# Second mixture of experts by indirect DMA, in 32-row blocks with the weights kept per column; the first norm in another order

## The chip, the cores and the metric

One core of one Trainium2 chip runs the whole program in one launch. The metric is the device time of the core in microseconds (us); lower is better. The time before is 2169.39 us, the median of three runs (2168.69 to 2171.74).

## The reference

Two transformer-like blocks run one after the other on 512 tokens of width 1024, all in float32. The first has an adaptive norm, a bidirectional mLSTM with a Fourier branch, and 16 experts that each choose 64 tokens. The second has a convolution branch, gated attention, cross attention and a mixture of 16 small experts in 4 groups; a last norm ends it. What the change touches is the start of the first block, and the mixture and the last norm of the second:

```
# first block, once for ctx (256 tokens, the modulation of c_ctx) and once for x (512 tokens, that of c)
mx = silu(c) @ w_ada + b_ada                     # 6 x 1024: shift, scale, gate, shift, scale, gate
px = (rmsnorm(x, g_norm1) * (1 + sc1) + sh1) @ w_in

# second block, last part: h = rmsnorm(x), 512 x 1024
p_group = softmax(h @ wg + bg);  g_star = argmax(p_group)           # one of 4 groups
p_exp = softmax(e_logits of that group);  top_v, top_i = top_k(p_exp, 2)
weights = p_group[g_star] * top_v / sum(top_v)                      # 2 experts of 16 for a token
a = h @ w_gate[e];  b = h @ w_up[e]                                 # 1024 x 256 each
y = sum over the two experts of (silu(a) * b * weight) @ w_down[e]  # 256 x 1024
out = rmsnorm(x + y, norm_final_g)
```

So 1024 pairs of a token and an expert are to be computed. An expert has 3 MB of weights (gate, up and down of 1 MB each), the 16 of them 48 MB.

## The kernel before

The order of the work on each engine is written out by hand, with semaphores between the engines. TensorE (PE) does all products, ScalarE (ACT) and VectorE (DVE) empty the PSUM banks, SyncE (SP) issues nearly all loads. The weights stream through `ring`, four slots of 2 MB (`weight_slots` in the profile). A slot is loaded again when the stage that used it is done. In the profile "bank" is a PSUM bank, "R" a work area (R1 to R7, and R14 which is R1 to R4), "SM" another, "C" the area C0, "H" the normed activations and "xT" the residual, both with the features on the partitions. `product` (L1529) is the helper for every plain product, so the rows of that line belong to many stages and are told apart by their operands.

**Start.** PE turns ctx and x so that the features lie on the partitions (L1538, L1545). It computes the modulation in four parts of 512 columns, `ada(0)` to `ada(3)` (L1560: eight products, four side by side in strips of 32 rows), and sums and turns each part (L1569, `ada_sum`). DVE adds the bias (L954). Parts 0 and 1 are the shift, parts 2 and 3 the scale, so the gains (L973) wait for all four. Then DVE scales ctx and x (L983), each with the reciprocal root from `root_inverse` (L959), for which PE must have summed the squares (`wide_sum`, L574 and L577). ACT adds the shift (L620 for ctx, L623 for x). Ahead of that, ACT issues nine small loads (L607 to L614) that later stages need. The product with `w_in` for the keys (L1529, H and weight_slots, first 256 columns of ctx) needs the shifted ctx.

**Second mixture.** PE turns h back to tokens on the partitions (L2033). ACT copies it twice (L884, and rounded L885), and GpSimd (POOL) forms the rest (L1514), so that h is there as the sum of a high and a low part in the faster number format of one pass. DVE picks the experts and gives each pair of token and expert a place: blocks of 64 rows belong to one expert each, and 1024 pairs need at most 31 blocks. The loop then always runs 16 times (`NPAIR2`), two blocks at a time, whatever the routing. For each pair of blocks:

- the rows are gathered by products with a 0/1 matrix (`gather_blocks`, L1529 with `picks`, 16 products of 512 columns), and turned (L2065)
- gate and up together (512 columns) are multiplied with the rows of both blocks side by side, in strips of 64 (L2099, 8 x 2 products); silu (L911, ACT) and the product with up (L1490, DVE); hidden turned (L2111)
- down (L2121, 4 x 2 products); the result is split in a high part (ACT, L924) and a low part (DVE, L1495)
- it is scattered to the tokens by products again (`scatter_tile`, L1529 with `GT_even` or `GT_odd`, 16 products) which stand between the gate and up products, and DVE adds it to xT (L1471, 8 additions)
- DVE makes the 0/1 matrix of the blocks to come (L1447, L1450) and the weights (L1456, L1458), and PE turns those (L2091)

SP reads the numbers of the experts from `block_expert` (L492) and loads the weights of each block (L498, L503) even where the expert stays the same. Gate and up are two blocks ahead in the ring, in runs of 1 KB; down is not double buffered. After the loop the last norm n6 runs over the partitions (L574, L577, L582, L585), PE turns the result (L2137), ACT copies it (L928), and SP writes it out (L537).

## Time and profile before

| | us |
|---|---|
| median of the runs | 2169.39 |
| profiled execution | 2166.3 |
| its span, first to last instruction | 2164.4 |
| PE busy in the span | 1996.4 |
| DVE, ACT, POOL busy | 733.9, 470.2, 12.6 |
| mean granted TensorE clock | 0.959 of full |

### The profile page before, as it was taken

To read this page: it belongs to the slowest core of one execution; us is meant where nothing else is said; L and a number is where in the kernel's file an instruction comes from. 1 tells how busy PE (TensorE), PEld (TensorE's weight loads), DVE (VectorE), ACT (ScalarE), POOL (GpSimd) and SP (SyncE) were. 2 spreads that over 40 slices of the span, in tenths; PEclk is the share of its full clock that TensorE was granted. 3 is DMA by queue.
4 is the path that set the end of the run, shared out by engine and by line. 5 is a ranking of instruction groups with operands and counts; after the bars stand their busy time and mean duration, and the time that the engine had idled before them with its cause. 6 is when DMAs were issued, how large, how long until landed. Compare 5 with 4: busy or idle time off the path is not lost.

```text
span 2164.4 us, 19621 instructions
## 1 busy us (share of the span) xinstructions
PE 1996.4 (92%) x7415; PEld 921.1 (43%) x7415; DVE 733.9 (34%) x1355; ACT 470.2 (22%) x845; POOL 12.6 (1%) x17
## 2 busy tenths in 40 slices
PE   6899999999899999999997997899997859999997
PEld 3544545544364444344433442344444334444443
DVE  3606205521231111111113695210212255455554
ACT  3211114420211110010112006530003222323223
POOL 0000000000000000000000000000000020000000
PEclk7999999999999999999998997999998969999999
DMA  9111443113238999999980211111200048878862
GB/s 371 28 66 39 173 177 136 39 59 117 78 122 349 422 417 419 422 422 422 423 345 18 72 66 39 40 39 62 72 22 0 0 151 289 296 273 288 293 233 78
DMA packets 151110, 399.03 MB, mean 184 GB/s; under 512 B 9284, under 2 KB 75156, under 8 KB 142868
## 3 DMA queue, kind: packets, MB, share of 16 engines
q1 hardware_dynamic: 144636, 393.40, 48.0%
q10 hardware_dynamic: 6424, 4.94, 0.7%
q8 instruction: 33, 0.54, 0.1%
q14 instruction: 17, 0.14, 0.0%
HBM read 396.23 MB, written 2.10 MB: 184 GB/s over the span
## 4 chain that ended last, share of the span: by engine, by line
PE 88%; DVE 4%; ACT 3%; issue 1%; DMA 1%; SPq 0%; DVEq 0%; ACTq 0%
PE bank L1529 49%; PE bank L1852 10%; PE bank L2099 6%; PE bank L1876 5%; PE bank L1827 3%; PE bank L1898 3%; PE bank L2121 3%; DVE SM L582 1%; PE bank L574 1%; PE bank L1980 1%; PE bank L2065 1%; PE bank L1605 1%; PE bank L1727 1%; PE bank L1560 1%; DMA weight_slots<-in_expert_w_up 1%
## 5 line engine op out<-in xcount | busy, mean ns | idle before, releaser
L1529 PE MATMUL bank<-H,weight_slots 128*128 128x512 f32 (+1 forms) x1088 | 450.0, 574 | 13.7 <-ACT H L620 12.5
L1529 PEld LDWEIGHTS bank<-H,weight_slots 128*128 128x128 f32 x1088 | 208.9, 193 | 252.6 <-issue 247.3
L1529 PE MATMUL bank<-R,weight_slots 128*128 128x512 f32 x576 | 249.1, 593 | 4.4 <-DVE R L1158 2.1
L1529 PEld LDWEIGHTS bank<-R,weight_slots 128*128 128x128 f32 x576 | 109.0, 190 | 141.6 <-issue 134.6
L1852 PE MATMUL bank<-weight_slots,SM 128*64 128x512 f32 x640 | 141.8, 593 | 6.8 <-DVE xT L1221 6.8
L2099 PE MATMUL bank<-weight_slots,SM 128*64 128x512 f32 x512 | 136.3, 622 | 5.6 <-DMA weight_slots<-in_expert_w_up 5.6
L1471 DVE TENSOR_TENSOR xT<-xT,bank 128x512 f32<-128x512 f32 x136 | 91.6, 686 | 78.8 <-PE bank L1529 78.8
L1876 PE MATMUL bank<-weight_slots,SM 128*64 128x512 f32 x384 | 111.6, 594 | 0.0
L1529 PE MATMUL bank<-R 128*128 128x128 f32 (+2 forms) x784 | 103.3, 287 | 3.2 <-ACT R L874 2.1
L1529 PEld LDWEIGHTS bank<-R 128*128 128x128 f32 x784 | 94.2, 195 | 7.1 <-issue 4.6
L1852 PEld LDWEIGHTS bank<-weight_slots,SM 128*64 128x64 f32 x640 | 45.4, 137 | 100.1 <-issue 86.7
L1231 DVE TENSOR_TENSOR R<-SM,bank 128x512 f32<-128x512 f32 x16 | 11.0, 686 | 212.8 <-PE bank L1852 212.8
L1529 PE MATMUL bank<-weight_slots,H 128*128 128x512 f32 x192 | 82.9, 592 | 0.0
L1260 DVE SCALAR_TENSOR_TENSOR R<-R,vec 128x512 f32<-128x512 f32 x120 | 79.6, 740 | 0.0
L1827 PE MATMUL bank<-R 128*128 128x512 f32 x144 | 71.0, 618 | 0.9 <-ACT R L762 0.9
L563 ACT ACTIVATE H<-xT 128x512 f32<-128x512 f32 x56 | 33.6, 626 | 175.7 <-DVE xT L1329 107.5
L1898 PE MATMUL bank<-H,weight_slots 128*128 128x512 f32 x128 | 59.3, 627 | 10.3 <-DVE H L585 10.3
L1876 PEld LDWEIGHTS bank<-weight_slots,SM 128*64 128x64 f32 x384 | 35.2, 137 | 69.9 <-issue 69.9
L1221 DVE SCALAR_TENSOR_TENSOR xT<-bank,mods,xT 128x512 f32<-128x512 f32 x72 | 54.1, 751 | 17.9 <-PE bank L1827 14.0
L1529 PE MATMUL bank<-h_high,picks 128*128 128x512 f32 x136 | 55.1, 405 | 4.8 <-DVE picks L1450 4.8
L2121 PE MATMUL bank<-R 128*64 128x512 f32 x256 | 58.5, 598 | 0.0
L1852 PE MATMUL bank<-R,SM 128*64 128x512 f32 x256 | 57.7, 592 | 0.8 <-ACT SM L744 0.8
(386 smaller groups left out, 2057.0 us busy)
## 6 DMA issues: line engine op xcount, KB each, us to landing
weight_slots<-in_w_up_e SPq DMA_DIRECT2D x24, 2048.0 KB, 12.7
weight_slots<-in_w_down_e SPq DMA_DIRECT2D x24, 2048.0 KB, 20.8
weight_slots<-in_w_in SPq DMA_DIRECT2D x18, 2048.0 KB, 10.2
weight_slots<-in_w_gate_e SPq DMA_DIRECT2D x16, 2048.0 KB, 11.8
weight_slots<-in_expert_w_gate SPq DMA_DIRECT2D x32, 1024.0 KB, 10.0
weight_slots<-in_expert_w_up SPq DMA_DIRECT2D x32, 1024.0 KB, 11.7
R<-in_expert_w_down SPq DMA_DIRECT2D x32, 1024.0 KB, 8.3
weight_slots<-in_w_ada SPq DMA_DIRECT2D x12, 2048.0 KB, 10.3
```

The costliest lines, as they stand in the source:

```text
L563: act.activation(H[:, k, 0:T], xT[:, k, :], ACT.Square).then_inc(sem("rms_sq"), 1)
L574: nc.tensor.matmul(part_bank[32 * g:32 * g + 32, :], ones[:, 0:32], H[:, k, 0:T], start=(k < 4), stop=(k >= 4), tile_position=(0, 32 * g)) ...
L1221: nc.vector.scalar_tensor_tensor(out=xT[:, j, :], in0=PS[2 + j % 2][:, :], scalar=mods[:, 40 + j, 0:1], in1=xT[:, j, :], op0=ALU.mult, op1 ...
L1260: nc.vector.scalar_tensor_tensor(out=cT[:, k, :], in0=u_pad[:, k, tap:tap + T], scalar=v("dw_w", KH * tap + k), in1=cT[:, k, :], op0=ALU.m ...
L1471: nc.vector.tensor_tensor(xT[:, j, :], xT[:, j, :], PS[3 + j % 2][:, :], ALU.add).then_inc(sem("x5"), 1)
L1529: ins = nc.tensor.matmul(dst, lhsT, rhs, start=(i == 0), stop=(i == len(pairs) - 1))
L1827: nc.tensor.matmul(PS[2 + j % 2][:, :], ypair[:, 128 * j:128 * (j + 1)], GT, start=True, stop=True).then_inc(sem("sc_mm"), 1)
L1852: ins = nc.tensor.matmul(b[64 * half:64 * half + 64, :], xs[:, 4 * rows + k, 64 * e:64 * e + 64], w[:, k, 512 * half:512 * half + 512], st ...
L1876: ins = nc.tensor.matmul(PS[6 + half][64 * e:64 * e + 64, :], hidT[:, e, k, 64 * rows:64 * rows + 64], w[e][:, k, 512 * half:512 * half + ...
L1898: ins = nc.tensor.matmul(banks[j][:, :], w[:, i, 128 * j:128 * (j + 1)], act_in(i), start=(i == 0), stop=(i == k - 1))
L2099: ins = nc.tensor.matmul(PS[2][BLK * i:BLK * (i + 1), :], xb[:, k, BLK * i:BLK * (i + 1)], ring[:, 2 * odd + i, 512 * k:512 * (k + 1)], st ...
L2121: ins = nc.tensor.matmul(PS[6 + half][BLK * i:BLK * (i + 1), :], hbT[:, f, BLK * i:BLK * (i + 1)], down2[:, c:c + 512], start=(f == 0), st ...
```

## The change

**Start.** The parts of the modulation are loaded and computed in the order scale, scale, shift, shift (`ADA_CHUNK`). The gains come after the first two, ctx is scaled right then, and the squares of x are summed on PE between `ada(1)` and `ada(2)`. ACT adds the shift of ctx to tiles 0 to 3 once the first shift part is there. The nine small loads go from the ACT queue to the SP queue, ahead of the ninth weight load.

On PE, at the start of the program, the piece of the difference from the first `ada` product (before L1560, after L1612) to the keys (L1529, L1581) reads as follows, first before and then after; L1569 and L1621 are `ada_sum`, L574 and L577 or L612 and L615 the sum of the squares of x:

```order
L1560 MATMUL bank<-weight_slots,silu_c 32x512 x16
L1569 MATMUL bank<-const,R 128x2 x4
L1560 MATMUL bank<-weight_slots,silu_c 32x512 x8
L1569 MATMUL bank<-const,R 128x2 x4
L1560 MATMUL bank<-weight_slots,silu_c 32x512 x8
L1569 MATMUL bank<-const,R 128x2 x8
L574 MATMUL bank<-H,const 32x512 x8
L577 MATMUL bank<-SM,const 128x512
L1529 MATMUL bank<-H,weight_slots 128x256 x32
```

```order
L1612 MATMUL bank<-weight_slots,silu_c 32x512 x16
L1621 MATMUL bank<-const,R 128x2 x8
L612 MATMUL bank<-H,const 32x512 x8
L615 MATMUL bank<-SM,const 128x512
L1612 MATMUL bank<-weight_slots,silu_c 32x512 x16
L1621 MATMUL bank<-const,R 128x2 x8
L1581 MATMUL bank<-H,weight_slots 128x256 x32
```

The sum of the squares of x has moved from behind the last part to the middle, ahead of the third part. On ACT, the nine small loads are gone from between the root of x (L567) and the shift of ctx (L620, now L648, which waits for the third and fourth part instead of the gains).

**Second mixture.** A block now has 32 rows, and 1024 pairs need at most 47 blocks. There are 4 columns of 12 blocks; step q of 12 (`NQUAD`) computes block q of every column, four blocks side by side in strips of 32. The blocks of an expert follow each other in a column, and group g starts at the head of column g where the room allows it. For each step:

- h is written to HBM once (`h2_rows`, four writes of 512 KB on the ACT queue), and POOL gathers the 128 rows of a step (512 KB) by indirect DMA. The 12 gathers have 12 buffers; at most two are on their way. The 0/1 products, the high and low parts and the scatter products are gone
- PE turns the rows (L2122), DVE copies them; gate and up are 8 x 4 products of 512 columns (L2140), down 4 x 4 (L2154); both work as before otherwise
- the result, times the weight of its row, is written to HBM (`y_rows`, 512 KB a step, ACT queue). At the end POOL adds it to the residual (turned to tokens before the loop, `x_tok2`) by indirect DMAs with an addition, eight of 512 KB; the second four each wait for the first of the same tokens
- the last norm runs on tokens: ACT squares and sums, DVE scales, SP writes four times 512 KB

**Weights kept per column.** A slot of the ring belongs to a column. Gate and up of an expert are one transfer of 1 MB each, in runs of 8 KB. They are issued for every step, but with a condition (`cond=changed`): no bytes are to move where the expert of the column stays. A step's loads are issued only after the gate and up products of the step before, since there is one slot a column; those of down after the down products before. The first four experts (0, 4, 8, 12) are loaded before the routing is known, and replaced where they were wrong.

On PE, inside the loop, the end of a pair of blocks before, behind its gate and up products (L1529: last of the 16 gathering products; L2111 turns the hidden rows, L2065 the gathered ones, L2121 is down):

```order
L1529 MATMUL bank<-h_high,picks 128x512
L1529 MATMUL bank<-h_low,picks 128x512
L2111 MATMUL bank<-const,R 128x128 x2
L2063 REGISTER_ALU
L2065 MATMUL bank<-const,C 128x128 x4
L2063 REGISTER_ALU
L2065 MATMUL bank<-const,C 128x128 x4
L2116 ISA
L2121 MATMUL bank<-R 64x512 x8
```

A whole step after (L2140 gate and up, L2130 hidden turned, L2122 gathered rows turned, L2154 down of the step before):

```order
L2140 MATMUL bank<-weight_slots,SM 32x512 x16
L2130 MATMUL bank<-const,R 128x128 x2
L2140 MATMUL bank<-weight_slots,SM 32x512 x16
L2122 MATMUL bank<-const,R 128x128 x8
L2154 MATMUL bank<-R 32x512 x16
```

Between the gate and up products of two steps there is now only the turning of the next rows and a down product.

On SP, the loads of one pair of blocks before:

```order
L498 ISA [waits b_gate_up]
L498 DMA weight_slots<-in_expert_w_gate 128x8x256
L498 DMA weight_slots<-in_expert_w_up 128x8x256
L498 ISA
L498 DMA weight_slots<-in_expert_w_gate 128x8x256
L498 DMA weight_slots<-in_expert_w_up 128x8x256
L503 ISA [waits b_down]
L503 DMA R<-in_expert_w_down 128x2x1024
```

And of one step after, from its second column on, with the four of down (which are those of the step before) at the end:

```order
L533 DMA weight_slots<-in_expert_w_gate 128x2048
L533 DMA weight_slots<-in_expert_w_up 128x2048
L533 ISA
L533 DMA weight_slots<-in_expert_w_gate 128x2048
L533 DMA weight_slots<-in_expert_w_up 128x2048
L533 ISA
L533 DMA weight_slots<-in_expert_w_gate 128x2048
L533 DMA weight_slots<-in_expert_w_up 128x2048
L537 DMA R<-in_expert_w_down 128x2048 [waits down_halves]
L537 DMA R<-in_expert_w_down 128x2048 x3
```

Eight conditional transfers of gate and up stand in a step where four unconditional ones stood, and they are for the step that comes next, not for the one after it. Ahead of them SP loads eight registers (expert and change of each column) where it loaded four.

The core of the diff:

```
-BLK = 64
+BLK = 32
+NQUAD = -(-((2 * T + E2 * (BLK - 1)) // BLK) // 4)
+ADA_CHUNK = (2, 3, 0, 1, 4, 5, 6, 7, 8, 9, 10, 11)
...
+            def load_half(i, j, expert, changed=None):
+                src = A[("expert_w_gate_2", "expert_w_up_2")[j]][0].rearrange("e (p k) n -> p e k n", p=P)[:, expert, :, :]
+                sp.dma_start(ring_jk[i][:, j:j + 1, :, :], src, cond=changed).then_inc(sem(f"half{j}_in"), 16)
...
+            for q in range(1, NQUAD + 1):
+                ago = here
+                if q < NQUAD:
+                    here = [block_of_step(q, i) for i in range(NSLOT)]
+                    sp.wait_ge(sem("gate_up_halves"), 2 * q)
+                    for i in range(NSLOT):
+                        for j in range(2):
+                            load_half(i, j, *here[i])
+                if q > 1:
+                    sp.wait_ge(sem("down_halves"), 2 * (q - 1))
+                for i in range(1 if q == 1 else 0, NSLOT):
+                    load_down(i, *ago[i])
...
+            for a in range(2):
+                for t in range(TT):
+                    if a:
+                        pool.wait_ge(sem(f"sum_in{t}"), 16)
+                    nc.gpsimd.indirect_dma_start(x_tok2[:, t, :], None, y_rows, bass.IndirectOffsetOnAxis(ap=token_slot[...], axis=0),
+                                                 compute_op=ALU.add).then_inc(sem(f"sum_in{t}"), 16)
...
+            for q in range(NQUAD):
+                pe.wait_ge(sem("q_xb"), 2 * (q + 1))
+                if q >= 2:
+                    pe.wait_ge(sem("q_hid"), q - 1)
+                gate_up(q, 0)
+                if q:
+                    turn_hidden(q - 1)
+                gate_up(q, 1)
+                if q + 1 < NQUAD:
+                    turn_rows(q + 1)
+                if q:
+                    down(q - 1)
+            turn_hidden(NQUAD - 1)
+            down(NQUAD - 1)
```

## Rows read from the trace of the kernel before

**Rows 1.** Page, part 2: the span in 40 slices of 54.1 us.
```profile
PE   6899999999899999999997997899997859999997
...
PEclk7999999999999999999998997999998969999999
...
GB/s 371 28 66 39 173 177 136 39 59 117 78 122 349 422 417 419 422 422 422 423 345 18 72 66 39 40 39 62 72 22 0 0 151 289 296 273 288 293 233 78
```

**Rows 2.** Chain that ended last, 1700 us on: start, length, what.
```profile
1801.74 1.87 PE bank L2099 x8
...
1823.98 1.87 PE bank L2099 x8
...
2131.27 3.61 PE bank L2121 x16
```

**Rows 3.** Groups, 1690 us on: line, engine, operands, count | busy us, mean ns | idle.
```profile
L2099 PE MATMUL bank<-weight_slots,SM 128*64 128x512 f32 x512 | 136.3, 622 | 5.6 <-DMA weight_slots<-in_expert_w_up 5.6
...
L2121 PE MATMUL bank<-R 128*64 128x512 f32 x256 | 58.5, 598 | 0.0
L1529 PE MATMUL bank<-h_high,picks 128*128 128x512 f32 x136 | 55.1, 405 | 4.8 <-DVE picks L1450 4.8
...
L2065 PE MATMUL bank<-const,C 128*128 128x128 f32 x136 | 21.3, 279 | 0.8 <-ACT C L896 0.3
```

**Rows 4.** Timeline of the start: start, length, engine, what [idle before it].
```profile
30.03 1.92 PE L1560 MATMUL bank<-weight_slots,silu_c 128*32 128x512 f32 x16 [0.82 <-DMA weight_slots<-in_w_ada]
...
35.44 3.64 PE L1560 MATMUL bank<-weight_slots,silu_c 128*32 128x512 f32 x16 [2.50 <-DMA weight_slots<-in_w_ada]
...
39.01 3.57 PE L1569 MATMUL bank<-const,R 128*128 128x2 f32 x16
...
49.06 0.50 ACTq L607 DMA_DIRECT2D rowb<-in_b_gates  x1
...
49.77 3.35 DVE L959 RECIPROCAL R<-SM 128x512 f32<-128x512 f32 x1 [3.21 <-ACT SM L567]
...
58.09 3.30 ACT L620 ACTIVATE H<-H,mods 128x256 f32<-128x256 f32 x8 [8.35 <-DVE H L983]
...
61.54 13.73 PE L1529 MATMUL bank<-H,weight_slots 128*128 128x256 f32 x55 [12.52 <-ACT H L620]
```

**Rows 5.** Timeline of PE: the first gate and up products; down and squares at the end.
```profile
1777.34 3.68 PE L2099 MATMUL bank<-weight_slots,SM 128*64 128x512 f32 x8 [5.57 <-DMA weight_slots<-in_expert_w_up]
...
1819.74 3.65 PE L2121 MATMUL bank<-R 128*64 128x512 f32 x16
...
1823.91 1.94 PE L2099 MATMUL bank<-weight_slots,SM 128*64 128x512 f32 x8
...
2142.26 1.92 PE L574 MATMUL bank<-H,const 128*32 128x512 f32 x16 [0.82 <-issue]
```

**Rows 6.** SP queue: one block's gate and up; register loads of L492 (ns min/median/max).
```profile
1791.65 0.37 SPq L498 DMA_DIRECT2D weight_slots<-in_expert_w_gate  x1
1792.11 0.53 SPq L498 DMA_DIRECT2D weight_slots<-in_expert_w_up  x1
...
L492 SPq TENSOR_LOAD <-block_expert x62: 262/264/471, 1759.0 to 2092.3; - x62
```

**Rows 7.** DMA issues of the page: KB each, median us from issue to landing.
```profile
R<-in_ctx ACTq DMA_DIRECT2D x1, 1024.0 KB, 5.9
...
wsmall<-in_w_in ACTq DMA_DIRECT2D x1, 64.0 KB, 6.9
...
out<-R SPq DMA_DIRECT2D x8, 256.0 KB, 2.0
```

**Rows 8.** Timeline of DVE: two steps of the routing before.
```profile
1758.75 0.17 DVE L1428 TENSOR_SCALAR block_expert<-bank 1x32 int32<-1x32 f32 x1
...
1762.14 1.29 DVE L1447 TENSOR_TENSOR SM<-R 128x512 f32<-128x512 f32 x2
```

More of the change, by code:

```diff
@@ L118, in constant_tables @@
     table[:, 962:982] = i % 32 == np.arange(20)[None, :]
+    table[:, 982:986] = i + P * np.arange(TT)[None, :]
+    group, other = i // EPG, np.arange(NG)[None, :]
+    table[:, 986:990] = i < EPG * other
+    table[:, 990] = 1.0
+    table[:, 991:995] = np.where(other <= group, NQUAD * other, -1e9)
+    table[:, 995:999] = EPG * other
     n, m = np.arange(T // 2)[:, None], np.arange(T)[None, :]
@@ L331, in build @@
         over = R7[0:E2, 3088:3088 + T // BLK]
[L332 to L334 removed]
+        nblk, ends, blk_base, shift, room = (R7[0:E2, 3104 + i:3105 + i] for i in range(5))
+        shifts = R7[0:E2, 3110:3110 + NG]
+        begun = R7[0:E2, 3116:3116 + 4 * NQUAD]
+        expert_row = R7[0:1, 3168:3168 + 4 * NQUAD]
+        expert_prev = R7[0:1, 3220:3220 + 4 * NQUAD]
@@ new lines, in _ @@
+            users = [(n_two + n) % NSLOT for n in range(len(W2))]
+            for i in range(NSLOT):
+                last = W2[max(n for n in range(len(W2)) if users[n] == i)]
+                sp.wait_ge(*reached(last[2], last[3]))
+                for half in range(2):
+                    load_half(i, half, slice(EPG * i, EPG * i + 1))
+            for i in range(NSLOT):
+                load_down(i, slice(EPG * i, EPG * i + 1))
+            sp.dma_start(g_out, A["norm_final_g_2"].rearrange("(a n) -> a n", a=1).broadcast_to([P, D])).then_inc(sem("g_out_in"), 16)
@@ new lines, in _ @@
+            for q in range(NQUAD):
+                if q:
+                    hidden_turned(q - 1)
+                silu(q)
+                if q:
+                    y_out(q - 1)
+            hidden_turned(NQUAD - 1)
+            y_out(NQUAD - 1)
+            for t in range(TT):
+                act.wait_ge(sem(f"sum_in{t}"), 32)
+                act.activation(last_sq, x_tok2[:, t, :], ACT.Square, accum_out=out_ss[:, t:t + 1]).then_inc(sem("out_sq"), 1)
+                act.wait_ge(sem("out_sq"), t + 1)
+                act.activation(out_std[:, t:t + 1], out_ss[:, t:t + 1], ACT.Sqrt, bias=small[:, 40:41], scale=1.0 / D).then_inc(sem("out_root"), 1)
@@ new lines, in _ @@
+            for q in range(NQUAD):
+                if q + 1 < NQUAD:
+                    x_turned(q + 1)
+                hidden(q)
+            dve.wait_ge(sem("g_out_in"), 16)
+            for t in range(TT):
+                dve.wait_ge(sem("out_root"), t + 1)
+                nc.vector.reciprocal(out_rstd[:, t:t + 1], out_std[:, t:t + 1]).then_inc(sem("out_inverse"), 1)
+                dve.wait_ge(sem("out_inverse"), t + 1)
+                nc.vector.scalar_tensor_tensor(out=out_tok[:, t, :], in0=x_tok2[:, t, :], scalar=out_rstd[:, t:t + 1], in1=g_out,
+                                               op0=ALU.mult, op1=ALU.mult).then_inc(sem("out_ready"), 1)
@@ new lines, in down @@
+            def down(q):
+                pe.wait_ge(sem("down_in"), 16 * (4 * (q + 2) - 1))
+                pe.wait_ge(sem("q_hidT"), q + 1)
+                if q:
+                    pe.wait_ge(sem("q_y"), 2 * q)
+                for half in range(2):
+                    for f in range(2):
+                        c = 1024 * f + 512 * half
+                        for i in range(4):
+                            r = slice(BLK * i, BLK * (i + 1))
+                            ins = nc.tensor.matmul(PS[6 + half][r, :], hbT[:, f, r], down_s[:, i, c:c + 512], start=(f == 0), stop=(f == 1), tile_position=(0, BLK * i))
+                    ins.then_inc(sem("down_halves"), 1)
```

521 lines of the change are left out of this document (242 added, 279 removed).

## The prediction

> **What bounds the kernel now.** I read the page's slices first [rows 1]. The second mixture is the last eight slices or so: PE is busy throughout, at the full clock, while the DMA engines move 273 to 296 GB/s where they reach 422 elsewhere. So in this loop PE is the bound and not the weights. The first slice has PE at six tenths with a clock below full; something waits there. The chain of waits then gives the period of the loop [rows 2]: gate and up of one pair of blocks start at 1801.74, of the next at 1823.98, so 22.2 us a pair and 16 of them. From the first gate and up product at 1777.34 [rows 5] to the end of the last down at 2131.27 + 3.61 = 2134.9 [rows 2] it is 357.6 us. Behind that the last scatter, the norm and the output take 29.5 us to the end of the span (2164.4, in the table). The groups show what fills the period [rows 3]: gate and up 136 us, down 58.5, and gathering by products 55.1 for the high parts alone.
>
> The timeline of the start [rows 4] has the other place: the key product waits 12.52 us and starts at 61.54, for the shift of ctx, which ACT begins at 58.09. The modulation was ready by 43. ACT was issuing its nine small loads, from 49.06 on, behind the root of x.
>
> **How often weights change.** The trace cannot say it; the loop before loads always. I ran the reference's router on its inputs for three seeds: 27 to 112 pairs an expert, 37 to 41 blocks of 32. Laid into the four columns, each seed gives 14 changes of an expert, one of them at step 0 and 13 in steps 1 to 11. Of one seed the steps are 1, 3, 2, 1, 1, 1, 1, 2, 0, 1, 0 columns. I sum with these; the other two spread the 13 alike.
>
> **The start.** The order is now: two parts, squares of x, two parts. The sums of squares run from about 29.5 and end near 35; the reciprocal of x (3.35 us) [rows 4] stands on DVE ahead of the copies of the last two parts, so these end near 41; PE's sums of both take up to 3.57 at the half clock, the bias 0.5, and ACT then shifts the last four tiles in half of 3.30. That makes 46.5 for the key product in place of 61.54: 15 us less (12 if more of it is at the half clock, 19 if the weights' arrival at 35.44 alone decides). What follows on PE is a chain of products, so the 15 us carry through. The nine loads on SP stand behind the eighth weight load, are 6.9 us each at most [rows 7], and are used after the value product; I cost them at nothing, and up to 6.9 us if they hold up the ninth weight load.
>
> **From the routing to the first gate and up.** Before, the table of experts is written at 1758.75 and the products start at 1777.34. After, 7 more small DVE steps at 0.2 us (the table step is 0.17 [rows 8]) make 1.4; the steps to the places are the same 2.2; then five wide steps of 2568 elements together, at 1.29 us for 1024 [rows 8], with small ones: 4.9. The index product is 16 matmul rows, about 3 us at the price of those in [rows 4]. The first gather is 512 KB; in its shadow PE turns the residual, 32 transposes at 21.3/136 = 0.157 us [rows 3], 5.0 us. Then turning and copying the rows 2.0, and the product for the row weights 3. Sum: 1780.5, 3 us later than before. The first weights are there: 12 MB (30 us at 422 GB/s) are started when the cross attention has used its slots, and the reload of one column begins near 1767 and takes 5 us.
>
> **The loop.** A strip of 32 rows is in the trace: 8 products, two rounds of four strips, take 1.92 us [rows 5]; four rounds of two strips of 64 take 3.65. So a round is 0.9 us whatever the width of its strips, and four blocks cost what two cost. Gate and up are 8 rounds, 7.2 us; down 4 rounds, 3.6; turning the rows 8 x 0.157 = 1.3; hidden 0.3. PE alone would need 12.4 us a step.
>
> But a column has one slot. From the end of a step's gate and up, PE has 1.3 + 3.6 = 4.9 us of other work; the weights of the next step must be issued, and land, in that time. For SP, eight issues at 0.45 us (0.37 and 0.53 [rows 6]) are 3.6 us. The landing of a small transfer is 1.4 us: 256 KB take 2.0 [rows 7], of which 0.6 are bytes at 422 GB/s. So a step without a change takes 5.0. With n changed columns it is 1.9 + 5.0 n: 2.1 MB at 422 GB/s [rows 1] are 5.0 us. A skipped transfer is not in the trace; it may cost nothing or its full issue, and I take the issue. The 8 register loads with their arithmetic (0.264 us each [rows 6], 0.66 with it) are 5.3 us and fit beside the 7.2 us of gate and up. Down's weights are issued behind the gate and up loads and are needed 8.5 us after those have landed, and fit.
>
> Sum over steps 1 to 11: 2 x 5.0 + 6 x 6.9 + 2 x 11.9 + 16.9 = 92.1, and 11 x 7.5 = 82.5. The first step adds 7.2, the end (two downs and the last hidden) 8.9, the gathers' 6 MB beside the first loads 5. After idle times of 5 us PE comes back at the half clock: behind 5.57 us of waiting the same eight rows take 3.68 us, and 1.94 in the loop [rows 5]. I charge 1.7 us four times, 7. The loop is then 203 us, 154.6 less than 357.6.
>
> The row that speaks against this is that pair, and the Trainium skill, "TensorE: Matmul & The Clock Gate", HAM oscillation, describes a kernel that waits for its next tile of weights at every tile and starts each one throttled. This kernel now has that form. By that rule every step would be cold (the second rival); the trace so far shows it only for waits of 5 us, with 2.50 us of waiting also followed by the half clock once [rows 4].
>
> **The tail.** ACT scales both halves 1.3, the last write to HBM is 512 KB, 2.6 us (the row of 256 KB and 0.6 more). Then eight indirect DMAs with an addition. None is in the trace. From below each costs its bytes, 1.2 us; from above 6.9, the dearest landing there is, of a load in runs of 64 B [rows 7]; 5.9 for the 1 MB of ctx lies between. I take 2.6, nearest to the 256 KB row, one behind the other: 20.8. The norm and the write of the last 128 tokens are 5.6. Together 30.3, against 29.5: 0.8 more. By the same bounds the tail is 19 to 65.
>
> The Trainium skill, "DMA: Bandwidth & Descriptors", Anatomy of one DMA (SWDGE path), gives a fixed 2.0 us and the bytes at 436 GB/s for a DMA that POOL issues, 3.2 us for these. By that estimate the tail would be 5 us longer. No run here shows it yet.
>
> **The sum.** -15 + 3 - 154.6 + 0.8 = -165.8. The profiled execution took 2166.3 (1.9 above its span), so 2000.5; the median of the runs is 3.1 above that execution: 2003.6, and I say 2004.
>
> **The rivals.**
>
> 1. Forecast, 0.67: as above, 2004.
> 2. Cold at every step, 0.08. Each gate and up takes 14.4 us in place of 7.2: 11 x 7.2 less the 7 charged, +72: 2076. For it: the half clock behind 2.50 us. Against: PE has 12 us of dense work in each step and mostly waits 2.
> 3. Waits hidden, 0.07. Skips cost nothing and the transfers overlap the down products so that 4.9 us a step is all: 54 in place of 92.1 + 5 + 7, -50: 1954. Against: the bytes of 9 of 11 steps alone are longer.
> 4. Indirect DMAs are dear, 0.15. At 6.9 us the eight of the tail are 55, +34, and the first gather is 2 us longer than what covers it: 2040. The other gathers stay hidden up to 16 us each, the length of a step.
> 5. The weights are not kept, 0.03: the condition costs the transfer anyway. 12.6 MB a step are 29.8 us at 422 GB/s, of which down's 9.9 lie beside gate and up (7.5) and leave 2.4; a step is 2.4 + 1.9 + 19.9 + 7.5 + 1.7 = 33.4, the loop 11 x 33.4 + 7.2 + 16 = 390, +187: 2191, slower than before. It decides from 15 us a step beyond the forecast, 6.4 MB.
>
> **Range and chances.** The forecast and rival 4 with their own bounds lie in 1965 to 2065; rival 3 is half in if I reach to 1955, rivals 2 and 5 (0.11) stay out. The range is 1955 to 2065. A change of 0.2%, 4 us, is about what a measurement here can tell from none. All cases but the fifth are faster by far more: faster 0.96, same 0.01, slower 0.03.
>
> **What would show it.** In the profile after: the key product starts near 46 and no small loads stand before it on ACT. The gate and up rows (L2140) take 7.2 us a step (64 matmul rows), and the idle time ahead of them is put down to DMA of gate or up, about 2 us in most steps and 7 to 12 in two to four. The expert weights that are moved are 18 times 3 MB (the first four and 14 changes), 54 MB, not 96. The period is 12.5 to 24 us and not constant. On POOL, indirect DMAs of the gathers run ahead of PE, and the last eight take about 21 us after the last write of `y_rows`. The prediction is wrong if the period is the same in every step (rival 5, or SP's own issue time is the bound), if L2140 rows are at the half clock throughout, or if PE waits for gathered rows (L2122) inside the loop.

## The result, and the profile after

The changed kernel takes 2027.11 us (median of 4 runs, 2023.41 to 2030.46). Its ratio to the kernel before, run beside it, is 0.934 (0.932 to 0.936), so it is about 6.6% faster. The forecast was 2004, in a range of 1955 to 2065. The profiled execution took 2030.46, with a span of 2028.7; the forecast on that basis was 2000.5, so 30 us of the expected gain did not come. The four executions lie 7 us apart and the profiled one is the slowest of them: in what follows, a few us of the whole time prove nothing by themselves, and the stages of the traces have to bear the argument.

Slices of 50.7 us of the page after, which answer to [rows 1]:

```profile
PE   6998999999989999999999799788999888457782
...
PEclk8998999999999999999999899889999988777886
...
GB/s 369 84 42 48 180 165 142 26 87 59 124 83 277 374 415 419 420 421 419 423 422 368 13 83 84 41 1 42 65 59 83 42 42 175 219 259 270 209 156 175
```

The loop (from the 35th slice on) now has PE at 4 to 8 tenths with a clock of 0.7 to 0.8, and the DMA engines are no fuller than before. Neither is the bound for long; they take turns.

The groups of the loop, for [rows 3]:

```profile
L2140 PE MATMUL bank<-weight_slots,SM 128*32 128x512 f32 x768 | 106.5, 705 | 70.5 <-DMA weight_slots<-in_expert_w_up 70.5
L2154 PE MATMUL bank<-R 128*32 128x512 f32 x384 | 43.7, 595 | 2.5 <-ACT R L937 1.3 <-DMA R<-in_expert_w_down 1.2
```

PE waits 70.5 us for weights of gate and up, and one such row takes 705 ns where one of down, the same form, takes 595.

The start, for [rows 4] (start, length, engine, what, idle before it and what ended it):

```profile
34.68 3.35 DVE L994 RECIPROCAL R<-SM 128x512 f32<-128x512 f32 x1 [0.64 <-ACT SM L605]
...
38.63 1.95 PE L1621 MATMUL bank<-const,R 128*128 128x2 f32 x16 [1.12 <-DVE R L983]
...
39.99 3.30 ACT L648 ACTIVATE H<-H,mods 128x256 f32<-128x256 f32 x8 [5.34 <-DVE mods L989]
...
43.44 6.77 PE L1581 MATMUL bank<-H,weight_slots 128*128 128x256 f32 x20 [2.85 <-ACT H L648]
```

The key product starts 18.1 us earlier than at 61.54. At 1700 us the same place of the program is 16.85 us ahead.

PE in the first steps and in one of a single changed column, for [rows 5]:

```profile
1755.85 7.07 PE L2140 MATMUL bank<-weight_slots,SM 128*32 128x512 f32 x64
...
1777.54 5.78 PE L2140 MATMUL bank<-weight_slots,SM 128*32 128x512 f32 x32 [13.60 <-DMA weight_slots<-in_expert_w_up]
...
1807.23 6.29 PE L2140 MATMUL bank<-weight_slots,SM 128*32 128x512 f32 x32 [15.37 <-DMA weight_slots<-in_expert_w_up]
...
1855.86 3.64 PE L2140 MATMUL bank<-weight_slots,SM 128*32 128x512 f32 x32
1859.43 1.09 PE L2122 MATMUL bank<-const,R 128*128 128x128 f32 x8
1860.45 3.64 PE L2154 MATMUL bank<-R 128*32 128x512 f32 x32
1868.30 6.48 PE L2140 MATMUL bank<-weight_slots,SM 128*32 128x512 f32 x32 [4.21 <-DMA weight_slots<-in_expert_w_up]
...
1976.41 3.62 PE L2140 MATMUL bank<-weight_slots,SM 128*32 128x512 f32 x32
...
1989.09 3.64 PE L2154 MATMUL bank<-R 128*32 128x512 f32 x32 [1.33 <-ACT R L937]
```

The first gate and up product starts at 1755.85, the last down ends at 1989.09 + 3.64 = 1992.7: the loop is 236.9 us. Behind a wait, the first half of gate and up takes 5.2 to 6.5 us; without one (1976.41) it takes 3.62. The 13.60 us of the first wait belong to a single changed column too, but there the last gathers move beside its weights.

SP's queue in the same step, for [rows 6], and what the DMA engines move then (columns: stretch, busy us and instructions of PE, PEld, DVE, ACT, POOL, granted clock, DMA share, GB/s):

```profile
1860.86 0.34 SPq L533 DMA_DIRECT2D weight_slots<-in_expert_w_gate  x1
1861.30 0.38 SPq L533 DMA_DIRECT2D weight_slots<-in_expert_w_up  x1
1861.96 0.08 SPq L533 DMA_DIRECT2D weight_slots<-in_expert_w_gate  x1
```

```profile
1861.00:1862.00 1.00, 1.00 (x16) 0.30 (x12) 0.95 (x2) 0.00 (x0) 0.00 (x0) 1.00 0.58 66
1862.00:1863.00 1.00, 1.00 (x12) 0.26 (x8) 0.00 (x0) 0.49 (x1) 0.00 (x0) 1.00 0.54 156
1863.00:1864.00 1.00, 1.00 (x12) 0.13 (x4) 0.00 (x0) 0.19 (x1) 0.00 (x0) 1.00 1.01 418
...
1867.00:1868.00 1.00, 0.00 (x0) 0.00 (x0) 0.00 (x0) 0.00 (x0) 0.00 (x0) 0.62 1.06 344
1868.00:1869.00 1.00, 0.70 (x4) 0.23 (x8) 0.00 (x0) 0.00 (x0) 0.00 (x0) 0.50 1.03 344
```

A transfer whose condition is false costs SP 0.07 to 0.09 us in the loop, a real one mostly 0.34 to 0.38 (some up to 0.65). In this step only the third column changes. Its gate is issued 1.4 us after the end of gate and up (1859.50), the full rate is reached at 1863, 3.5 us after it, and 2.1 MB need another 5. PE has been idle since 1864.1; when its products start at 1868.30, the granted clock is 0.50.

The tail, timeline:

```profile
1993.51 0.33 ACTq L948 DMA_DIRECT2D y_rows<-R  x1
1996.90 1.55 POOL L1565 DMA_INDIRECT H<-y_rows,token_slot  x1 [214.78 <-DMA y_rows<-R]
...
2022.62 1.06 ACT L960 ACTIVATE SM<-H 128x1024 f32<-128x1024 f32 x1 [1.01 <-DMA H<-y_rows,token_slot]
```

From 1992.7 to the end of the span it is 36.0 us. The eight additions run from 1996.90 to 2022.62, 25.7 us. From issue to landing one takes 9.7 us (median in the list of DMA issues).

By stage, after against before in the spans: start -16.85, from there to the first gate and up -4.65 (1777.34 less 1755.85 is 21.5), loop 236.9 - 357.6 = -120.7, tail 36.0 - 29.5 = +6.5. That is -135.7, as the spans say (2164.4 to 2028.7).

### The profile page after: what moved, and what is told of

The parts are those of the page before. It is cut to its first block, busy times and chain, and to the rows that moved or that the text cites. A ratio compares the mean times of both kernels' runs of the same rounds, so it can differ in the third digit from the quotient of the medians.

```text
span 2028.7 us, 18210 instructions
## 1 busy us (share of the span) xinstructions
PE 1785.7 (88%) x7159; PEld 810.7 (40%) x7159; DVE 559.8 (28%) x1100; ACT 391.1 (19%) x708; POOL 24.7 (1%) x26
## 4 chain that ended last, share of the span: by engine, by line
PE 83%; DMA 5%; DVE 5%; ACT 4%; issue 2%; SPq 1%; POOL 0%; ACTq 0%; DVEq 0%; POOLq 0%
PE bank L1581 45%; PE bank L1904 11%; PE bank L1928 5%; PE bank L2140 5%; DMA weight_slots<-in_expert_w_up 4%; PE bank L1879 3%; PE bank L1950 3%; PE bank L1612 1%; PE bank L612 1%; DMA H<-y_rows,token_slot 1%; SPq L533 1%; PE bank L2032 1%; DVE SM L620 1%; PE bank L1779 1%; PE bank L2154 1%
## 5 line engine op out<-in xcount | busy, mean ns | idle before, releaser
L1581 PE MATMUL bank<-H,weight_slots 128*128 128x512 f32 (+1 forms) x1088 | 450.9, 575 | 4.1 <-ACT H L648 2.9
L1581 PEld LDWEIGHTS bank<-H,weight_slots 128*128 128x128 f32 x1088 | 209.3, 193 | 241.9 <-issue 236.3
L1581 PE MATMUL bank<-R,weight_slots 128*128 128x512 f32 x576 | 250.8, 596 | 4.4 <-DVE R L1195 2.1
L2140 PE MATMUL bank<-weight_slots,SM 128*32 128x512 f32 x768 | 106.5, 705 | 70.5 <-DMA weight_slots<-in_expert_w_up 70.5
L1581 PEld LDWEIGHTS bank<-R,weight_slots 128*128 128x128 f32 x576 | 109.6, 191 | 142.6 <-issue 135.7
L1904 PE MATMUL bank<-weight_slots,SM 128*64 128x512 f32 x640 | 141.8, 593 | 6.8 <-DVE xT L1258 6.8
L1928 PE MATMUL bank<-weight_slots,SM 128*64 128x512 f32 x384 | 111.6, 594 | 0.0
L1581 PE MATMUL bank<-R 128*128 128x128 f32 (+2 forms) x784 | 103.3, 287 | 3.2 <-ACT R L902 2.1
L1581 PEld LDWEIGHTS bank<-R 128*128 128x128 f32 x784 | 94.2, 195 | 7.1 <-issue 4.6
L2140 PEld LDWEIGHTS bank<-weight_slots,SM 128*32 128x32 f32 x768 | 27.8, 127 | 138.7 <-issue 138.7
L1581 PE MATMUL bank<-weight_slots,H 128*128 128x512 f32 x192 | 82.9, 592 | 0.0
L1515 DVE COPY SM<-bank 128x512 f32<-128x512 f32 x24 | 15.5, 687 | 203.3 <-PE bank L2122 195.9
L601 ACT ACTIVATE H<-xT 128x512 f32<-128x512 f32 x48 | 28.7, 625 | 175.0 <-DVE xT L1366 107.5
L1258 DVE SCALAR_TENSOR_TENSOR xT<-bank,mods,xT 128x512 f32<-128x512 f32 x72 | 54.1, 751 | 17.8 <-PE bank L1879 13.9
L1928 PE MATMUL bank<-H,SM 128*64 128x512 f32 x128 | 56.2, 592 | 0.0
```

The lines of the kernel that those rows point to most:

```text
L601: act.activation(H[:, k, 0:T], xT[:, k, :], ACT.Square).then_inc(sem("rms_sq"), 1)
L1258: nc.vector.scalar_tensor_tensor(out=xT[:, j, :], in0=PS[2 + j % 2][:, :], scalar=mods[:, 40 + j, 0:1], in1=xT[:, j, :], op0=ALU.mult, op1 ...
L1581: ins = nc.tensor.matmul(dst, lhsT, rhs, start=(i == 0), stop=(i == len(pairs) - 1))
L1904: ins = nc.tensor.matmul(b[64 * half:64 * half + 64, :], xs[:, 4 * rows + k, 64 * e:64 * e + 64], w[:, k, 512 * half:512 * half + 512], st ...
L1928: ins = nc.tensor.matmul(PS[6 + half][64 * e:64 * e + 64, :], hidT[:, e, k, 64 * rows:64 * rows + 64], w[e][:, k, 512 * half:512 * half + ...
L2140: ins = nc.tensor.matmul(PS[2 + q % 2][r, :].rearrange("p (j n) -> p j n", j=2), xb[q % 2][:, k, r], ring_jk[i][:, :, k, :], start=(k == 0 ...
```

## The experiments

A single execution of a kernel is compared with the profiled execution of the changed kernel by its span (2028.7) and by its stages. Such a difference counts by the whole time only where it leaves the 7 us that the changed kernel's own executions span (2023.41 to 2030.46).

**The start: order or loads?** One kernel is the changed one with the nine small loads back on the ACT queue, where they stood before:

```
-            for n, (name, src, free, value) in enumerate(W):
-                if n == 2 * NSLOT:
-                    small_weights()          # the nine loads, on SP
...
+            act.dma_start(rowb[0:1, 0:16], ...)   # and eight more, ahead of the shift of ctx
```

> The changed kernel with the nine small loads back on the ACT queue, behind the root of x; all else as changed. Theory (the start's gain has two parts, the loads held ACT and the order made the scale late): ACT's loads take 8.5 us from about 34.7, so the shift of ctx starts near 43 and not 40, and the key product near 47 in place of 43.44, 3 to 4 us later; most of the 18.1 us come from the order. Rival (the loads alone are the gain): the key product is back near 58 to 61.

Measured: span 2040.4, 11.7 more. ACT in its timeline:

```profile
33.68 0.50 ACTq L632 DMA_DIRECT2D rowb<-in_b_gates  x1
...
36.21 5.72 ACTq L639 DMA_DIRECT2D wsmall<-in_w_in  x1
41.96 5.97 ACTq L639 DMA_DIRECT2D wsmall<-in_router_group_w  x1
47.96 5.93 ACTq L639 DMA_DIRECT2D wsmall<-in_router_expert_w  x1
54.00 3.30 ACT L645 ACTIVATE H<-H,mods 128x256 f32<-128x256 f32 x8 [19.53 <-issue]
```

The key product starts at 57.44, 14.0 us later; the expectation of 3 to 4 us, near 47, missed. The loads hold ACT's own queue from 33.7 to 53.9, though no engine waits for their data. That is over twice what they took before (49.06 to 58.0): here the DMA engines move 352 to 386 GB/s of weights all this time, there they had fallen to 75 GB/s by 57. The other kernel is the one before with the same nine loads moved to SP:

> The kernel before with only the nine small loads moved to the SP queue. Theory: ACT is free at 49.7, when the root of x is done, and the key product starts near 53 in place of 61.54: 8.4 us less, and the span is 8 us shorter. Rival (order alone is the gain): 61 again.

Measured: 2153.73, beside 2168.36 for the kernel before on the same chip: 14.6 less. The key product starts at 48.88. That is 12.7 us earlier where 8.4 were expected. The squares of x, in the kernel before and then in this one:

```profile
42.51 3.64 PE L574 MATMUL bank<-H,const 128*32 128x512 f32 x16
```

```profile
40.89 1.93 PE L587 MATMUL bank<-H,const 128*32 128x512 f32 x16
```

They run at a granted clock of 0.50 before and of 1.00 here, and the root of x ends at 45.55 in place of 49.74. Until 43 us, when SP reaches the small loads, the two kernels do the same work, so these 4.2 us come from the clock of the one execution and not from the edit. What the loads cost the kernel before is the rest, 8.4 us: ACT held from 49.74 to 58.09. The new order alone brings 4.1 (61.54 to 57.44). In the changed kernel the loads would cost 14.0, probably because they would meet full DMA engines (no run changes that alone): the order brings its whole gain only with the loads out of ACT's way.

**The loop: what the reloads cost.** In one kernel no expert is ever replaced (it computes with the first four experts' weights throughout), in the other every column is reloaded at every step:

```
-  tensor_tensor(expert_change[:, :], expert_row, expert_prev, ALU.not_equal)
+  tensor_tensor(expert_change[:, :], expert_row, expert_row, ALU.not_equal)   # never
+  tensor_tensor(expert_change[:, :], expert_row, expert_row, ALU.is_equal)    # always
```

> The changed kernel with the table of changes all zero, so that no weights are replaced in the loop (it computes with the first four experts' weights). It leaves out the replaced transfers and nothing else. Theory (what the loop takes above PE's own work is the bytes of replaced weights and the half clock behind the waits): steps of 12.0 us without idle time ahead of gate and up, the loop 146 us in place of 237, the time near 1936. Rival (the issue of eight conditional loads or their skipping holds each step): an idle time of 1 us or more stays in each step, the loop 160 us or more.

> The changed kernel with the table of changes all one, so that every column's weights are transferred in every step. It prices the condition. Theory (a transfer whose condition is false moves nothing, one that is true costs its bytes): 12.6 MB a step, steps of 33 to 38 us, the loop 390 to 440 us, the time 2180 to 2230, slower than the kernel before. Rival (keeping the weights is worth little since other waits would take its place): under 2100.

Measured: 1938.0 (span 1936.2) and 2217.12 (span 2215.3). The group of gate and up, first never, then always replaced:

```profile
L2140 PE MATMUL bank<-weight_slots,SM 128*32 128x512 f32 x768 | 86.9, 594 | 1.2 <-DMA weight_slots<-in_expert_w_up 1.2
```

```profile
L2140 PE MATMUL bank<-weight_slots,SM 128*32 128x512 f32 x768 | 111.4, 733 | 230.1 <-DMA weight_slots<-in_expert_w_up 230.1
```

With no replacement a step is 12.0 us, the loop 145.3, and a row takes the 594 ns of the full clock. The reloads of the changed kernel therefore cost about 91 us. Without the condition the changed kernel would be 49 us slower than the one before: keeping the weights is worth some 190 us and is what makes the change pay. (Of the 190, some 13 fall on the last down product, which waits 14.05 us for its own weights there and 1.33 in the changed kernel.)

**Down's weights.** The reloads of down are left out (so its products use the first experts):

```
-                for i in range(1 if q == 1 else 0, NSLOT):
-                    load_down(i, *ago[i])
```

> The changed kernel without the loads of down inside the loop (it keeps the first four experts' down weights). Theory A (down's bytes and the writes of y_rows run beside those of gate and up and share the DMA engines, which makes the wait with one changed column 4.2 us and not the 2.0 forecast): idle time ahead of gate and up falls from 70.5 us to 50 to 60, that of a step with one change to about 2.5. Theory B (down's transfers stand behind gate and up in the queue and cost nothing; the landing itself is 2 us longer than I took): 70 us of idle time again, and 4 us in a step with one change.

Measured: 2025.16; PE idle before gate and up 69.1 us in place of 70.5. The loop is 3.2 us shorter (233.7), of which 1.4 are in this wait and 1.2 in the one wait for down that the changed kernel has (at 1955.30). Down's megabyte a column costs next to nothing here: it is hidden behind gate and up, as the forecast had it.

**The half clock.** PE is given four products that nothing reads, behind each down:

```
                     down(q - 1)
+                    for _ in range(4):
+                        nc.tensor.matmul(PS[4][:, :], ident, const[:, 0:512], start=True, stop=True)
```

> The changed kernel with four more f32 products of 512 columns on PE (3.4 us) behind each down of the loop, into a bank that nobody reads. Theory A (a wait of 4 us brings PE back at the half clock, which costs 1.6 to 2.9 us in the first half of gate and up): the idle time in steps with one change falls to about 0.8 us, their first halves take 3.6 us in place of 5.2 to 6.5, and the two steps without a wait are 3.4 us longer, so the loop is 3 to 7 us shorter. Theory B (the longer first halves are something else, such as the transfers in progress at that time): the first halves stay above 5 us and the loop is 5 to 7 us longer.

Measured: 2027.42, span 2025.6: 3.1 less, which the whole time can't tell from none. One step with a single change:

```profile
1862.95 3.70 PE L2177 MATMUL bank<-const 128*128 128x512 f32 x8
1867.40 3.64 PE L2140 MATMUL bank<-weight_slots,SM 128*32 128x512 f32 x32 [0.75 <-DMA weight_slots<-in_expert_w_up]
```

The first half takes 3.64 in place of 6.48, so the half clock comes from PE's idling and not from the new weights. The full clock is worth more than the 3.1 us: over the four steps of one changed column in a row (from 1850.32 to 1931.68 in the changed kernel, from 1850.85 to 1923.02 here) it saves 9.2 us. In the steps without a wait and behind the last one the extra products themselves stand in the way and cost most of that again (3.3, 2.0 and 2.7 us). In steps with two or three changes four products do not fill the gap, and the halves still take 5.1 to 6.3 us.

**When the transfers may start.** Gate and up of an expert are each split in two halves of the contraction; the first halves are issued when PE has finished with the first half of the old weights, 4 us earlier, and PE starts when they are there. SP also reads the registers of a step ahead of time, between the second halves and the loads of down:

```
-                    sp.wait_ge(sem("gate_up_halves"), 2 * q)
-                    for i in range(NSLOT):
-                        for j in range(2):
-                            load_half(i, j, *here[i])
+                    for half in range(2):
+                        sp.wait_ge(sem("gate_up_halves"), 2 * q - 1 + half)
+                        for i in range(NSLOT):
+                            load_half(i, half, *here[i])
+                if q + 1 < NQUAD:
+                    ahead = [block_of_step(q + 1, i) for i in range(NSLOT)]
...
             def gate_up(q, half):
+                pe.wait_ge(sem(f"half{half}_in"), 16 * (8 * (q + 2) - 2))
```

> The changed kernel with gate and up loaded in two halves of the contraction (features 0 to 3 and 4 to 7 of each partition, in runs of 4 KB): the first half of the next step is issued when the first half of this step's products is done. Theory A (the wait is the transfer less what PE has beside it): 3.6 us more lie beside the first half and 3.6 beside the second, so one or two changed columns are hidden whole; idle time ahead of gate and up falls from 70.5 to 12 to 25 us, the half clock's share with it, and the time is 1945 to 1970. Theory B (the DMA engines are the bound of the loop by their bytes, or twice as many issues on SP): over 2000.

Measured: 1981.94 (4 runs, 1979.75 to 1986.24), ratio to before 0.914 (0.913 to 0.916). Groups of its loop:

```profile
L2142 PE MATMUL bank<-weight_slots,SM 128*32 128x512 f32 x768 | 92.9, 628 | 23.8 <-DMA weight_slots<-in_expert_w_up 23.8
L2156 PE MATMUL bank<-R 128*32 128x512 f32 x384 | 46.8, 631 | 12.3 <-DMA R<-in_expert_w_down 10.9 <-ACT R L941 1.3
```

The longest of its waits for down (the granted clock is 0.50 from 1825 to 1829):

```profile
1827.12 5.10 PE L2156 MATMUL bank<-R 128*32 128x512 f32 x32 [6.30 <-DMA R<-in_expert_w_down]
```

The idle time before gate and up fell by 46.7 us, as expected, but the time came out 12 above the expected 1945 to 1970. The second row has what the expectation missed: down now waits 10.9 us for its own weights, whose reload stands behind gate and up on SP and was covered by the longer wait before; behind two of these waits it also runs at the half clock (5.10 and 5.34 us in place of 3.64). Part of it is the edit's own doing: for the wait shown, PE had released the old weights at 1811.9 and SP's last load of gate and up was out at 1810.6, but the loads of down were issued from 1816.11 on, behind the eight register loads. No run separates the two.

**The tail: is it the addition?** The same eight indirect DMAs without `compute_op=ALU.add` (rows overwrite the residual, so the additions are left out):

> The changed kernel with the eight last indirect DMAs as plain gathers into the same places; the addition of the experts' result to the residual is left out. Theory A (the addition halves the rate: they move 190 to 213 GB/s): the eight take 10 to 12 us in place of 24, set by POOL's issue of 1.25 us each, and the tail behind the last down is 24 to 27 us in place of 36. Theory B (the rows of 4 KB from HBM at random places set the rate): the tail stays above 33 us.

Measured: 2020.07, below all executions of the changed kernel; its tail is 27.0 us (1991.2 to 2018.2) in place of 36.0. Two stretches of 2 us of the changed kernel, then one of this:

```profile
2002.00:2004.00 2.00, 0.00 (x0) 0.00 (x0) 0.00 (x0) 0.00 (x0) 1.67 (x2) 0.50 1.04 178
...
2008.00:2010.00 2.00, 0.00 (x0) 0.00 (x0) 0.00 (x0) 0.00 (x0) 0.00 (x0) 0.50 1.08 207
```

```profile
2000.00:2002.00 2.00, 0.00 (x0) 0.00 (x0) 0.00 (x0) 0.00 (x0) 0.99 (x2) 0.50 1.00 365
```

With the addition, fully busy DMA engines move about half the bytes, and POOL needs 1.54 us to issue one in place of 0.94.

A kernel that leaves nothing out gathers plainly and adds on VectorE. Its gathers go tile by tile, and none of them waits for another any more:

```
-    nc.gpsimd.indirect_dma_start(x_tok2[:, t, :], None, y_rows, ..., compute_op=ALU.add)
+    nc.gpsimd.indirect_dma_start(rows_in[(2, 8)[a] + t], None, y_rows, ...)
...
+    nc.vector.tensor_tensor(x_tok2[:, t, :], x_tok2[:, t, :], rows_in[(2, 8)[a] + t], ALU.add)
```

> The tail alone: the eight indirect DMAs that add the second experts' rows to x_tok2 become plain indirect gathers into free buffers, and VectorE adds the rows in sixteen operations of 128x512 (about 0.69 us each by L1366, 11 us in all, beside the later gathers), then goes on with the output norm. Nothing is left out. Theory A: the addition inside the transfer halves the rate (190 to 213 GB/s with it, 283 to 397 without, in the run that left it out), so the tail goes from 36.0 to 28 to 30 us and the time from 2027 to about 2020, 0.3% less. Theory B: the adds on VectorE and the hops between the engines take the place of the transfer; tail 33 to 37 us, time within 3 us of the changed kernel.

Measured: 2024.79 (4 runs, 2023.87 to 2025.3), ratio 0.9335 (0.932 to 0.935). By the trace its tail is 29.9 us (from 1989.56 + 3.64 = 1993.2 to 2023.1), 6.1 less; how much of that is the addition and how much the other order and the missing waits, no run separates. By the medians the gain is 2.3, and the two intervals overlap: on this kernel alone it is not settled by the times. The second theory was half right: from the second tile on VectorE sets the pace:

```profile
2008.27 1.23 DVE L1537 TENSOR_TENSOR H<-H,xT 128x1024 f32<-128x1024 f32 x1
...
2012.05 1.23 DVE L1537 TENSOR_TENSOR H<-H,xT 128x1024 f32<-128x1024 f32 x1
```

A tile takes 3.78 us there, about what two additions of 1.23, the reciprocal (0.15) and the scaling (1.29) add up to.

Both edits of the two last stretches together:

> Both in one: replacements of gate and up split into halves by rows of the contraction (k_halves, 1981.94) and the tail with plain gathers and adds on VectorE. If the two are independent, as theory A of the tail and the place of the two stretches say, the gains add: 1982 less 7, about 1975 (1971 to 1979), ratio to before 0.910 to 0.912. If the tail's gain is hidden by the last products or by VectorE, it stays at 1979 to 1984.

Measured: 1975.40 (5 runs, 1971.66 to 1978.07), ratio 0.9105 (0.9093 to 0.9118), which lies below the interval of the halves alone (0.9128 to 0.9158). Its tail is 30.0 us, against 35.1 with the additions in the DMA. Here the gain of the plain gathers stands out, and this is the fastest version that I ran: 51.7 us below the changed kernel.

**The small steps of the router.** Eight operations of POOL are put beside them again, on data that nothing reads:

```
+            for j in range(8):
+                pool.wait_ge(*reached("h2_ev", j + 1))
...
+                nc.gpsimd.tensor_tensor(R5[:, 1024:1536], R5[:, 512:1024], R5[:, 512:1024], ALU.subtract)
```

> The changed kernel with eight tensor_tensor operations of 128x512 put back on POOL beside the routing, on data that nothing reads: as the kernel before had there with its h_low (L1514, 9.88 us for the eight). Their only other effect is that the first gathers of middle rows are issued behind them, which has time to spare. In the trace of before, nine small operations of VectorE that lie beside that row took 7.21 us (4.21 + 1.19 + 1.81); in the trace of after the same nine took 1.75 us (0.78 + 0.17 + 0.80). Theory: a small operation of VectorE takes longer while POOL runs a tensor_tensor; then the nine come back to 5 to 7.5 us, the first gate/up moves from 1755.85 to about 1760, and the whole gets 4 to 6 us longer than the changed kernel (2032 to 2036). Rival: the steps were slow for another reason (another order of the start, waits on themselves); then they stay at 1.75 us and the time stays within 1.5 us of the changed kernel.

Measured: 2033.58, span 2031.8, 3.1 more; the first gate and up starts at 1760.88, 5.0 us later. The same nine operations of VectorE in three timelines: before, after, and in this kernel:

```profile
1740.09 9.88 POOL L1514 TENSOR_TENSOR h_low<-R,h_high 128x512 fp32r<-128x512 f32 x8 [5.09 <-ACT h_high L885]
...
1743.35 4.21 DVE L1362 TENSOR_TENSOR R<-R 128x16 f32<-128x16 f32 x4
1747.59 1.19 DVE L1372 COPY R<-R 128x4 f32<-128x4 f32 x1
1748.82 1.81 DVE L1362 TENSOR_TENSOR R<-R 128x12 f32<-128x12 f32 x4
```

```profile
1725.35 0.78 DVE L1399 TENSOR_TENSOR R<-R 128x16 f32<-128x16 f32 x4
1726.16 0.17 DVE L1409 COPY R<-R 128x4 f32<-128x4 f32 x1
1726.37 0.80 DVE L1399 TENSOR_TENSOR R<-R 128x12 f32<-128x12 f32 x4
```

```profile
1722.76 9.31 POOL L1550 TENSOR_TENSOR R<-R 128x512 f32<-128x512 f32 x8 [5.53 <-ACT R L911]
...
1726.95 1.80 DVE L1399 TENSOR_TENSOR R<-R 128x16 f32<-128x16 f32 x4
1728.78 0.95 DVE L1409 COPY R<-R 128x4 f32<-128x4 f32 x1
1729.77 2.33 DVE L1399 TENSOR_TENSOR R<-R 128x12 f32<-128x12 f32 x4
```

They take 7.2, 1.75 and 5.1 us: the theory holds by the stage and by the nine operations. The time of the single execution agrees (2032 to 2036 expected) but is too near the changed kernel's own to show it alone.

## Why the prediction was right, and where it missed

The direction, the size and the mechanism were right: the loop loses its gathering and scattering products and takes 12.0 us a step where no weights change, against the 12.4 forecast; the weights are moved only on a change; and the range held the time. By the steps:

- **Start**, forecast -15, came as -18.1 at the key product and -16.85 at 1700 us. The path was the one described, but the sum came this near by terms that partly cancel. The copies ended at 39.2 (41 in the forecast), and PE's sums took 1.95 at the full clock where I had up to 3.57 at the half; so the shift began at 39.99, where the forecast's terms put it near 45. Against that ACT shifted all eight tiles (3.30) ahead of the key product and not half of them, since both shift parts came at once. Where 1.2 us are lost again up to 1700 us is open.
- **Routing to the first gate and up**, forecast +3, was -4.65. I counted the steps that the change adds, at 0.17 us, and left those that it keeps at their old length. Nine of these had been stretched by POOL's work on `h_low`, which the change removes: 5.5 us (7.2 to 1.75), and the experiment that puts such work back moves the first product by 5.0. So this step was wrong, 7.65 us in the forecast's favour; some 2 us of it stay unexplained.
- **Loop**, forecast 203, was 236.9, and this is most of the miss. It splits by PE's timeline. (a) From the end of gate and up to the start of the next: 118.4 us over eleven steps, forecast 97.1 (92.1 and the 5 for the gathers). With one changed column it is 8.5 to 9.6 us (forecast 6.9), but 14.6 in step 1, beside the last gathers (6.9 and their 5; the DMA engines moved only 141 to 289 GB/s from 1763 to 1769 there), with two 14.6 and 15.3 (11.9), with three 20.0 (16.9), and with four, where all are always replaced, 24.3 to 25.3 (21.9). About 3.7 + 5.3 n describes them apart from step 1, where I had 1.9 + 5.0 n. The bytes at 422 GB/s were about right. The constant was wrong: I took 1.4 us of landing from the write of `out` [rows 7] and one issue (0.45), while the windows show the full rate only 3.5 us after the products' end. What it is made of is open: it is not the place in SP's queue, for with the first column changed, whose gate is out after 0.3 us, the gap is 9.2 and 9.6, no shorter than with the second or third (8.5 to 9.0). The two steps with none took 4.4 each (forecast 5.0), PE's own work between the products, since skipped transfers are cheap. (b) Gate and up themselves in these steps: 102.7 us, forecast 82.5 and 7 for the clock, so 13.2 more. I charged the half clock behind four long waits; the rows show it behind every one of the nine, down to a wait of 3.78 us. Against 3.62 + 3.64 + 0.3 a step it is 19.6 us in all. The experiment with products in the gap removed it where the gap was filled. (a) and (b) are 34.4 us together; the two ends and the rounding of the forecast take 0.5 off. The Trainium skill, "TensorE: Matmul & The Clock Gate", HAM oscillation, tells of this form, a start throttled at each wait for a tile: the trace agrees for every step that waits, and the second half of the step was at the full clock again each time.
- **Tail**, forecast 30.3, was 36.0. The eight additions took 25.7 in place of 20.8, that is 3.2 each where I had 2.6 from a plain write, and the last write's landing with POOL's start 3.4 in place of 2.6. The missing fact was the half rate with an addition, for which before had no row. The Trainium skill, "DMA: Bandwidth & Descriptors", Anatomy of one DMA (SWDGE path), gave an estimate of 3.2 us for each, which is what came out, but by chance: it is the length of one transfer, where one here took 9.7 from issue to landing with others on their way, and the same eight without the addition left the tail 9.0 us shorter.
- Down's reloads, the register loads (262 to 268 ns as before, though one took 1011), the gathers of the middle rows and the strips of 32 (0.9 us a round) cost what the forecast said. PE never waits for gathered rows.

These terms are -1.85, -7.65, +33.9 and +5.7: together 30.1, the whole difference of the profiled executions. It was luck that 9.5 us of unforeseen gain hid a part of 39.6 of unforeseen cost, though the range would have held without it. Of the signs named, the steps of the loop repeat after 13.7 to 29.7 us (12.5 to 24 forecast), and the wait with one changed column is 3.8 to 4.6 us and not about 2.

**The rivals.** Cold at every step (2076): true of nine steps of eleven, but only for their first half, so 20 us and not 79. Waits hidden (1954): not in this kernel, yet the halves show that most of the wait was a matter of when the transfers may start. Dear indirect DMAs (2040): 3.2 us each in the tail and not 6.9, so a seventh of that extra. Weights not kept (2191): refuted, and the always-replaced kernel shows that its price was about right (2217).

## What to carry to other kernels

With one buffer, a wait that is short of being covered costs three times: the latency from release to full rate, the bytes, and a TensorE at the half clock behind it. Splitting the buffer by the order in which it is consumed hid two thirds of it here (70.5 to 23.8 us) with no more memory; then look for what that wait had covered (here the loads of down, and the register loads ahead of them). When a change takes an engine's work away, look at what ran beside it too: a neighbour's rows may have been long because of it.

## What the runs showed of the hardware

- Indirect DMAs with an addition moved 172 to 213 GB/s in stretches of 2 us with the DMA engines fully busy, plain ones of the same rows 289 to 391. POOL issued one in 1.54 us, a plain one in 0.94.
- VectorE operations of 0.17 to 0.2 us took up to 1.2 us while POOL ran tensor_tensor of 128x512, seen before and in the experiment.
- A DMA with a false condition took its queue 0.07 to 0.09 us.
- Small loads in runs of 64 B and less held the queue that issued them up to 5.97 us each while the DMA engines were full with weights; the first two of them took 0.40 and 0.63, and the last one of the kernel before, with the DMA engines at 75 GB/s, 0.61. They were asynchronous for the data, not for the engine that issued them.
- In the loop of the changed kernel, each of TensorE's nine waits for gate and up (3.78 us and more) was followed by 5.2 to 6.5 us for what takes 3.6 at the full clock.
